# Third and fourth norm of a transformer block by token halves, with the sums of the following modulated norm among the products of a down projection

## What is computed

```
h = layer_norm(ALPHA*h + mix, ln2)
h = layer_norm(ALPHA*h + xa, ln3)                    # xa = cross attention @ wo
h = layer_norm(ALPHA*h + 0.5*swiglu(h, ffn2), ln4)   # 1024 -> 2816 -> 1024
```

```
h2 = rms_norm(h, norm_g) * (1 + scale) + shift       # scale, shift from a condition
z  = h2 @ w_in       # convolutions, neighbourhood attention and gates read it
```

## Time and profile before

| | |
|---|---|
| median of 3 runs | 1752.1 us (1751.47 to 1753.6) |
| profiled execution | 1754.92 us |
| its span | 1753.3 us |
| PE busy | 1719.0 us, 98% |
| DVE busy | 983.3 us, 56% |
| ACT busy | 681.0 us, 39% |
| POOL busy | 149.0 us, 8% |

### The profile page before, as it was taken

One profiled execution on the slowest core, in us unless ns is written; L12 is line 12 of the kernel. 1 busy time (PEld: TensorE's weight loads), 2 busy tenths in 40 slices (PEclk: granted clock), 3 DMA queues, 4 the chain that ended last, 5 costly groups with the idle time before them and its releaser, 6 DMA issues.

```text
span 1753.3 us, 22917 instructions
## 1 busy us (share of the span) xinstructions
PE 1719.0 (98%) x8534; PEld 1409.0 (80%) x8534; DVE 983.3 (56%) x1323; ACT 681.0 (39%) x961; POOL 149.0 (8%) x154
## 2 busy tenths in 40 slices
PE   8999999999999999999999999999999999999999
PEld 7888888788787788886888888876777777788887
DVE  4333339977964674457333333447967769744442
ACT  4222231245445465534222222235444545732221
POOL 0000000012004611012000000003011020000000
PEclk9999999999999999999999999999999999999999
DMA  5332347633221344223333333332332322143331
GB/s 198 96 97 95 99 140 235 221 97 116 73 73 53 128 135 154 61 73 96 101 97 98 98 96 100 96 105 67 92 98 70 96 83 81 61 132 108 108 99 70
DMA packets 50757, 183.87 MB, mean 105 GB/s; under 512 B 5696, under 2 KB 5952, under 8 KB 50304
## 3 DMA queue, kind: packets, MB, share of 16 engines
q1 hardware_dynamic: 44640, 161.50, 29.4%
q10 hardware_dynamic: 5040, 16.00, 2.8%
q0 software_dynamic: 1008, 5.41, 0.9%
HBM read 180.79 MB, written 2.10 MB: 104 GB/s over the span
## 4 chain that ended last, share of the span: by engine, by line
PE 84%; DVE 9%; ACT 2%; DMA 2%; issue 2%; POOL 0%; SPq 0%; ACTq 0%; DVEq 0%
PE proj L372 76%; DVE w_lo L364 2%; DVE ada_prod L1030 1%; DVE y L1851 1%; ACT w_hi L357 1%; PE aux L1696 1%; DMA ctxv<-ada_in 1%; DVE h L645 1%; PE aux L1683 1%; PE aux L1488 1%; PE proj L1509 1%; DMA ctxk<-ada_in 1%; PE aux L1673 1%; DMA h<-x_in 0%; DVE score L1123 0%
## 5 line engine op out<-in xcount | busy, mean ns | idle before, releaser
L364 DVE TENSOR_TENSOR w_lo<-raw,w_hi 128x1024 fp32r<-128x1024 f32 x303 | 383.0, 1265 | 418.4 <-ACT w_hi L357 411.5
L372 PE MATMUL proj<-a_hi,w_hi 128*128 128x512 f32 (+1 forms) x1536 | 603.0, 393 | 9.7 <-DVE a_lo L651 4.4
L372 PE MATMUL proj<-a_hi,w_lo 128*128 128x512 f32 (+1 forms) x1536 | 592.9, 386 | 0.0
L372 PE MATMUL proj<-a_lo,w_hi 128*128 128x512 f32 (+1 forms) x1536 | 592.6, 386 | 0.0
L357 ACT ACTIVATE w_hi<-raw 128x1024 fp32r<-128x1024 f32 x303 | 318.6, 1053 | 233.8 <-PE proj L372 170.8
L372 PEld LDWEIGHTS proj<-a_hi,w_hi 128*128 128x128 f32 x1536 | 289.6, 189 | 76.3 <-DVE a_lo L651 6.6
L372 PEld LDWEIGHTS proj<-a_lo,w_hi 128*128 128x128 f32 x1536 | 290.0, 189 | 58.9 <-issue 2.9
L372 PEld LDWEIGHTS proj<-a_hi,w_lo 128*128 128x128 f32 x1536 | 289.5, 189 | 58.6
L372 PE MATMUL proj<-hid_hi,w_hi 128*128 128x512 f32 (+1 forms) x374 | 142.2, 380 | 0.0
L372 PE MATMUL proj<-hid_hi,w_lo 128*128 128x512 f32 (+1 forms) x374 | 140.8, 377 | 0.0
L372 PE MATMUL proj<-hid_lo,w_hi 128*128 128x512 f32 (+1 forms) x374 | 140.8, 377 | 0.0
(11 more groups left out here) (342 smaller groups left out, 1999.5 us busy)
## 6 DMA issues: line engine op xcount, KB each, us to landing
raw<-stream SPq DMA_DIRECT2D x303, 512.0 KB, 3.5
ctxk<-ada_in ACTq DMA_DIRECT2D x12, 512.0 KB, 3.9
ctxv<-ada_in ACTq DMA_DIRECT2D x12, 512.0 KB, 4.2
out<-h ACTq DMA_DIRECT2D x8, 256.0 KB, 2.0
h<-x_in SPq DMA_DIRECT2D x3, 512.0 KB, 7.6
btab<-rpb_in POOLq DMA_DIRECT2D x4, 384.0 KB, 3.5
cond_row<-cond_in ACTq DMA_DIRECT2D x1, 1024.0 KB, 6.1
side<-mem_in POOLq DMA_DIRECT2D x1, 1024.0 KB, 5.2
```

The source lines that it names most:

```text
L364: nc.vector.tensor_tensor(w_lo[:, st.slot], raw[:, st.slot], w_hi[:, st.slot].bitcast(F32), ALU.subtract).then_inc(lo_ready, 1)
L372: mm = nc.tensor.matmul(dst, a, b, start=start and n == 0, stop=stop and n == 2)
```

## The change

`HALVED` becomes `[0, 4, 5, 6]`: LN3, LN4 and MODN by halves.

- LN3: the last strip of the output projection runs for half 0 and then half 1, with the opening of the sums and the moments of half 0 among the products of half 1; the moments of half 1 stand between the context value strips. The splits of six weight strips are spread anew over the steps of the norm on ACT and VectorE.
- The first four strips of the second feed-forward layer run staggered, half 0 with lags (0, 0, 1, 3), then half 1 with (0, 1, 3, 5).
- LN4: the last chunk of the down projection runs first whole for half 0 (three strips), then whole for half 1, and TensorE takes the first five sums of MODN's half 0 among the products of half 1. The splits of strips 1 and 2 of the next projection move behind that, `ahead=1`.
- MODN by halves: half 0 is normalised while LN4 of half 1 goes on; TensorE takes six of the eight sums of half 1 among the products of half 0 of the next four strips, and two behind them. These run staggered, lags (0, 0, 1, 5) and (0, 1, 3, 5). Their clock-keeping products go.
- `act_na` and `dve_na` split four strips ahead instead of three for j = 0 to 3, and none at j = 4.
- GpSimd adds LN4's shift in sixteen half instructions, each behind the square of its chunk.

The core of the diff:

```diff
-        HALVED = [0]
+        HALVED = [0, 4, 5, 6]
...
+        def act_mod_squares(act, b, lo, hi):
+            for c in range(lo, hi):
+                act.wait_ge(n_xn, LN4.c0 + KD * b + c + 1)
+                if c >= 2:
+                    act.wait_ge(n_stat, MODN.t0 + KD * b + c - 1)
+                nc.scalar.activation(sq[:, c % 2, tokens(b)], h[:, c, tokens(b)], ACT.Square,
+                                     bias=LN4.shift(c)).then_inc(n_sq, 1)
+
+        def pe_mod_stats(pe, b, lo, hi):
+            for c in range(lo, hi):
+                pe.wait_ge(n_sq, MODN.q0 + KD * b + c + 1)
+                nc.tensor.matmul(aux[:, 2 * b + 1, :HT], mean_d[:], sq[:, c % 2, tokens(b)], start=(c == 0),
+                                 stop=(c == KD - 1)).then_inc(n_stat, 1)
...
+        def dve_ln4(dve, b, lo, hi):
+
+            if lo == 0:
+                dve.wait_ge(n_std, LN4.s0 + 2 * b + 1)
+            for c in range(lo, hi):
+                dve.wait_ge(r_cent, 8 * LN4.u + KD * b + c + 1)
+                nc.vector.scalar_tensor_tensor(h[:, c, tokens(b)], h[:, c, tokens(b)], LN4.gain(c), rstd[:, tokens(b)],
+                                               ALU.mult, ALU.mult).then_inc(n_xn, 1)
+                if c + 2 < KD:
+                    dve_half_recentre(dve, LN4, b, c + 2)
+
+        def dve_mod(dve, b, lo, hi):
+
+            if lo == 0:
+                dve.wait_ge(n_std, LN4.s0 + 2 * b + 2)
+            for c in range(lo, hi):
+                if c < KD:
+                    dve.wait_ge(n_raw, LN4.r0 + KD * b + c + 1)
+                    nc.vector.scalar_tensor_tensor(hm[:, c, tokens(b)], h[:, c, tokens(b)], MODN.gain(c),
+                                                   rstd[:, tokens(b)], ALU.mult, ALU.mult).then_inc(mod_xn, 1)
+                if c >= 1:
+                    dve.wait_ge(n_hi, MODN.h0 + KD * b + c)
+                    nc.vector.scalar_tensor_tensor(a_lo[:, c - 1, tokens(b)], hm[:, c - 1, tokens(b)],
+                                                   MODN.shift(c - 1), a_hi[:, c - 1, tokens(b)].bitcast(F32), ALU.add,
+                                                   ALU.subtract).then_inc(n_lo, 1)
...
                 if first and quad:
-                    strip_two_pairs(pe, Nth(s0), Nth(g0), ready)
+                    strips_staggered(pe, Nth(s0), Nth(g0), 0, (0, 0, 1, 3), half_ready_of(pe, ready, 0))
+                    strips_staggered(pe, Nth(s0), Nth(g0), 1, (0, 1, 3, 5), half_ready_of(pe, ready, 1))
...
+            if sums:
+                half(0, 0)
+                half(0, 1)
+                pe_half_open(pe, m)
+                half(0, 2)
+                half(1, 0, {2: lambda: pe_half_mean(pe, m, 0), 4: lambda: pe_half_square(pe, m, 0)})
+                half(1, 1, {5: lambda: sums(0), 7: lambda: sums(1)})
+                half(1, 2, {1: lambda: sums(2), 3: lambda: sums(3), 5: lambda: sums(4)})
+                return
...
                 elif first and j == 0:
-                    strip_two_pairs(pe, st, g, lo_ready_of(pe, MODN))
+                    beside = {n: lambda c=n - 2: pe_mod_stats(pe, 1, c, c + 1) for n in range(2, KD)}
+                    strips_staggered(pe, st, g, 0, (0, 0, 1, 5), half_ready_of(pe, MODN, 0), beside)
+                    pe_mod_stats(pe, 1, KD - 2, KD)
+                    strips_staggered(pe, st, g, 1, (0, 1, 3, 5), half_ready_of(pe, MODN, 1))
...
-                if not first or j:
-                    split_hi(act, st.plus(3))
+                if not first or j != RING:
+                    split_hi(act, st.plus(RING if first and j < RING else 3))
...
+            split_hi(act, Nth(S_CTXV + 2))
+            act_half_square(act, LN3, 0)
+            act_half_mean_square(act, LN3, 0)
+            act_half_std(act, LN3, 0, chain)
+            act_half_hi(act, LN3, 0, 0, 1)
+            split_hi(act, Nth(S_CTXV + 3))
+            act_half_hi(act, LN3, 0, 1, 2)
+            act_half_square(act, LN3, 1)
+            act_half_hi(act, LN3, 0, 2, 3)
+            split_hi(act, Nth(S_FFN2))
+            act_half_mean_square(act, LN3, 1)
+            act_half_hi(act, LN3, 0, 3, 5)
+            split_hi(act, Nth(S_FFN2 + 1))
+            act_half_hi(act, LN3, 0, 5, 6)
+            act_half_std(act, LN3, 1, chain)
+            act_half_hi(act, LN3, 0, 6, 7)
+            split_hi(act, Nth(S_FFN2 + 2))
+            act_half_hi(act, LN3, 0, 7, KD)
             act_ctxv_take(act)
             split_hi(act, Nth(S_FFN2 + 3))
+            act_half_hi(act, LN3, 1, 0, KD)
...
+            for c in range(KD):
+                if c == 2:
+                    split_lo(dve, Nth(S_NA + 3))
+                dve_mod(dve, 0, c + 2, c + 3) if c + 2 <= KD else None
+                dve_ln4(dve, 1, c, c + 1)
+            dve_mod(dve, 1, 0, KD + 1)
...
+            pe_half_strip(pe, last, LN3.groups[KD - 1], 0, a_hi, a_lo, 0, KD, KD)
+            pe_half_strip(pe, last, LN3.groups[KD], 1, a_hi, a_lo, 0, KD, KD,
+                          {0: lambda: pe_half_open(pe, LN3), 3: lambda: pe_half_mean(pe, LN3, 0),
+                           5: lambda: pe_half_square(pe, LN3, 0)})
...
+            pe_down_halves(pe, S_DOWN2, G_DOWN2, KF, LN4, sums=lambda c: pe_mod_stats(pe, 0, c, c + 1))
+            pe_mod_stats(pe, 0, 5, KD)
+            pe_half_mean(pe, LN4, 1)
+            pe_half_square(pe, LN4, 1)
```

More of the change, by code:

```diff
@@ L446, in __init__ @@
                 self.s0 = sum(2 if n in HALVED else 1 for n in range(k))
-                self.c0 = 8 * self.s0
+                self.c0 = 8 * sum(2 if n in HALVED else 1 for n in range(k) if n != 6)
                 self.r = r
@@ L658, in act_hi, with pool_half_shift @@
                 nc.scalar.activation(m.hi[:, c], m.dst[:, c], ACT.Identity, bias=m.shift(c)).then_inc(n_hi, 1)
+        def pool_half_shift(pool, m, after):
+            for b in range(2):
+                for c in range(KD):
+                    pool.wait_ge(n_sq, after.q0 + KD * b + c + 1)
+                    nc.gpsimd.tensor_scalar(h[:, c, tokens(b)], h[:, c, tokens(b)], 1.0, m.shift(c), ALU.mult,
+                                            ALU.add).then_inc(n_raw, 1)
         def pool_shift(pool, m):
@@ L713, in half_ready_of, with pe_half_strip @@
             return lambda k: pe.wait_ge(n_lo, m.h0 + KD * b + k + 1)
-        def pe_half_strip(pe, st, g, b, xh, xl, first, blocks, beside=None):
+        def pe_half_strip(pe, st, g, b, xh, xl, first, blocks, total, beside=None):
             pe.wait_ge(lo_ready, st.n + 1)
@@ L833, in lo_ready_of, with act_mod_hi @@
+        def act_mod_hi(act, b, lo, hi):
+            for c in range(lo, hi):
+                act.wait_ge(mod_xn, KD * b + c + 1)
+                nc.scalar.activation(a_hi[:, c, tokens(b)], hm[:, c, tokens(b)], ACT.Identity,
+                                     bias=MODN.shift(c)).then_inc(n_hi, 1)
         def lo_ready_of(pe, m):
@@ L884, in two @@
                     st, g = Nth(s0 + j, 4, i), Nth(g0 + j, 4, i)
-                    if not (quad and first and j == 0):
+                    if not (quad and first):
                         split_hi(act, st.plus(3))
+                    elif j < 3:
+                        split_hi(act, st.plus(4))
                     if j % 2 == 0:
@@ L904, in two @@
                     st, g = Nth(s0 + j, 4, i), Nth(g0 + j, 4, i)
-                    if not (quad and first and j == 0):
+                    if not (quad and first):
                         split_lo(dve, st.plus(3))
+                    elif j < 3:
+                        split_lo(dve, st.plus(4))
                     if j % 2:
@@ L951, in hybrid_blocks, with act_down_seven @@
         LAST = DOWN_STRIPS * (KD - 1)
-        def act_down_halves(act, s0, m, chain, beside=None):
+        def act_down_seven(act, s0, m, beside=None, ahead=2):
             for a in range(LAST):
@@ L961, in act_down_halves @@
             act_square(act, m, KD - 2)
-            split_hi(act, Nth(s0 + LAST + 4))
+            if ahead == 2:
+                split_hi(act, Nth(s0 + LAST + 4))
+        def act_down_halves(act, s0, m, chain, beside=None):
+            act_down_seven(act, s0, m, beside)
             act_half_square(act, m, 0)
@@ L1878, in dve_na @@
                     norm(2 * (j - 7) + 1)
-                if not first or j:
-                    split_lo(dve, st.plus(3))
+                if not first or j != RING:
+                    split_lo(dve, st.plus(RING if first and j < RING else 3))
                 if j == 2:
@@ L2143, in _ @@
             act_ctxk_norm(act, chain)
-            for n in range(KD):
+            for n in range(KD - 1):
                 split_hi(act, Nth(S_XO + n + 3))
@@ L2163, in _ @@
[L2163 to L2169 removed]
+            act_down_seven(act, S_DOWN2, LN4, ahead=1)
+            act_half_square(act, LN4, 0)
+            act_half_mean_square(act, LN4, 0)
+            act_half_std(act, LN4, 0, chain)
@@ new lines, in _ @@
+            act_mod_squares(act, 0, 0, 2)
```

(18 more changed lines are left out.)

120 lines of the change are left out of this document (62 added, 58 removed).

## The result

The changed kernel takes 1767.55 us (median of 4 runs, 1763.66 to 1769.83), the kernel before beside it 1752.8: a ratio of 1.0083, 95% interval 1.0063 to 1.0102. It is slower by 14.75 us. Its profiled run took 1763.66 us (span 1761.9), the fastest of the four.

The account below looks back on a forecast made before the run. TensorE carries 84% of the chain, but VectorE's slackless chain from the end of strips 0 and 1 sets the kernel's end. Third norm +4.3 and fourth with modulated norm +9.5 sum to +13.8 us: median 1765.9, range 1753 to 1773.

Parts of the forecast that it names:

- both new waits: TensorE waits about 2 us on an add of squares in the output projection, over 3 us at feed-forward strip 2.
- Part one, +2.8 and the clock +1.5: Third norm by halves: late splits and buffer cost 2.8 us, low clock 1.5 (0 to 4.8), together +4.3.
- Part two, the gain: After the modulated norm, the first strip product comes at 1186.3 instead of 1196.89, ten microseconds earlier.
- Part two, half 1: Modulated norm's strips: TensorE idles 2.8 us, starts half 1 at 1207.8, then low clock adds 1.5 us.
- Up to `glu`: VectorE's chain behind the strips: `glu` stands at 1223.6 instead of 1214.44, +9.2 us.
- From `glu` to the scores: VectorE has one split less, -1.1 us, so the wait at 1241.1 moves to 1249.1, +8.0.
- Where TensorE would wait: At the turn behind the first score row, TensorE waits 4 us or more where it waited 0.95.
- (1): Both norm stages: same delays, but the clock stays up; +10.8 us, 1763; chance 0.17.
- (2): Fourth norm: VectorE loses 0.4 us at each of GpSimd's eight half 1 shifts; +3.2 us, 1769; chance 0.08.
- (3): Strips 2 and 3 of both quads: splits and squares reach TensorE in time; -4.5 us, 1747.6; chance 0.08.
- (4): VectorE's chain behind `glu` is absorbed, only the strips' end counts; +4.3 + 1.2 us, 1757.6; chance 0.12.
- (5): Whole kernel: gains and losses cancel within 3.5 us; chance 0.05.

Follow-up runs that it names:

- e1: Only the third norm by halves, the fourth and modulated norms as in the kernel before; 1755.32 us beside 1751.91, ratio 1.0021.
- e4: Changed kernel with the convolution's taps spread over later steps in the first pass; 1762.75 us, ratio 1.0063 to the kernel before.
- e6: Changed kernel with the last two sums of the modulated norm's half 1 among half 0's strip products; 1764.4 us, ratio 1.0064 to before.
- e7: Changed kernel with half 1 of the wide projection's first four strips as two pairs, not staggered; 1767.65 us, ratio 1.0085 to before.
- e9: Changed kernel with small clock-keeping products in TensorE's waits around the modulated norm, strips and first scores; 1764.34 us, ratio 1.0069 to before.
- e2: Only the fourth and modulated norms by halves, the third as in the kernel before; 1761.15 us, ratio 1.0056 to before.
- e12: Changed kernel with paired strips, later splits, earlier last sums, later taps and small clock-keeping products; 1749.27 us beside 1752.55 before, ratio 0.9981.
- e8: Kernel before with six extra VectorE products of nat and nsg ahead of `glu`, first pass only; 1758.06 us beside 1752.34, ratio 1.0030.
- e5: Third norm alone by halves, with half 0 of its four strips as two pairs; 1754.92 us beside 1752.34 before, ratio 1.0013.

## Why the prediction was right, point by point

**The time.** 1766 was predicted, 13.8 us more; measured were 1767.55 and 14.75. The mechanism was right: both new waits, the clock behind most of them, and VectorE's chain as what sets the end of part two. That the sum is so near is in part luck, since in both parts two terms are off in opposite ways, as follows.

**Part one, +2.8 and the clock +1.5.** In the change's own trace A is 3.06 longer, with no drop at the opening. Six profiles have the third norm as the change makes it (change, e1, e4, e6, e7, e9): A is 51.84 to 54.77, mean 53.13, so +4.35, where the prediction had +4.3. The wait at the opening was to be 2.1 and is 1.94; the first strip product was to come 22.65 us behind the chunk's start and comes at 22.68; the wait at strip 2 was to be 4.7 and is 4.52. Only the short wait at strip 3 isn't there. But the split of the sum was off. An estimate from the windows (the missing share of the clock times 4 us each) puts the low clock at 1.7 us in the change and e9, 3.4 in e1, e6 and e7 and 5.1 in e4, a mean of 3.1; without it A would be 49.7 to 50.2, 1.2 above the kernel before. So the walk's +2.8 was 1.6 too much and the clock's +1.5 was 1.6 too little. The run of this part alone, e1, measured +3.4.

**Part two, the gain.** First strip product at 1186.3 by the prediction, 25.15 us behind the chunk's start; measured 25.20. The waits ahead of the strips and at their second step, 1.3 and 0.7 us, are 0.67 and 0.75; the one for the fourth `a_lo`, 2.2, is 2.17.

**Part two, half 1.** The start of half 1 was predicted 46.65 us behind the chunk's start and is 47.93, the wait there 2.59 for 2.8. The step that was too small: I let the clock fall behind the wait at half 1 only, and it also fell behind the one at the fourth `a_lo`, 0.57 in the window from 1192.

**Up to `glu`.** Predicted +9.2, with the clock's 1.5 it is 10.7; measured +12.6. Half 1 slowed down as foreseen (0.67 in the window from 1208). What the sum lacked, beside the 1.3 us at the start of half 1, is GpSimd: its sums for the bias stretch the last split from 1.23 to 1.73 us.

**From `glu` to the scores.** Predicted 1.1 less, measured 2.8 less (86.91 - 65.89 = 21.02 against 23.78), since those same sums were over before most of the taps. The two misses, 1.9 too little and 1.7 too much, nearly cancel. GpSimd's sums are in both, but the 1.3 us of clock has nothing to do with the gain behind `glu`: that these two cancel is luck. The first turn was predicted +8.0 and 1.5 for the clock, and came +10.35 later; at the end of the stage it is +9.86, in e2 +8.64. Predicted: +9.5.

**Where TensorE would wait.** I had it wait some 4 us at the turn. It waits 3.43 at the first scores, half a strip earlier, because `nq` stands behind 14 taps on the same engine. The cause is the chain that I named (e4 takes 8 taps from ahead of `nq`, and the wait goes), the place was wrong. I also had not seen the 3.10 us for `nsq`, behind ScalarE's late `nat`; it is hidden like the rest of TensorE's delay, as e7 shows.

**The rivals.** (1), clock stays up: out, it fell behind the waits of 4.52, 2.59 and 3.43 us, and behind that of 2.17 where I had not put it; in this profile it stayed up behind the opening (1.94 us). e9 shows the price ahead of `glu`. (2), VectorE loses at GpSimd's half shifts: out. GpSimd's shift took 1.14 us beside VectorE and 0.48 alone, while VectorE kept its pace of 0.40 an operation. So the rule that the prediction set beside this rival, by which the one that starts second blocks fully, is not what these rows show:

```profile
1194.79 1.14 POOL L665 TENSOR_SCALAR h<-h,cols 128x256 f32<-128x256 f32 x1 [0.37 <-ACT sq L846]
...
1199.68 0.48 POOL L665 TENSOR_SCALAR h<-h,cols 128x256 f32<-128x256 f32 x1 [0.70 <-ACT sq L846]
```

```profile
1194.80 0.48 DVE L881 SCALAR_TENSOR_TENSOR a_lo<-hm,modv,a_hi 128x256 fp32r<-128x256 f32 x1
1195.20 0.48 DVE L865 SCALAR_TENSOR_TENSOR h<-h,cols,work 128x256 f32<-128x256 f32 x1
```

(3), all splits in time, -4.5: out for this order of work, but e12 shows that the idea could be had, at -3.3, with another order. (4), the chain is absorbed: out by e4 and e8. (5), the parts cancel: out by e1 and e2, both lose.

## What to carry to other kernels

Halving a norm brings the first product forward by as much as one expects, and the end of the strips that somebody is waiting for by nothing. Ask which product the next engine needs, and when the second half of that is done. A wait's releaser in a profile is the last to come; walk the order of the engine behind it before you move anything, or the next wait stands where the old one was (e5). And when a chain of one engine sets the time, look for work in it that can wait, here the taps of a convolution: moving them alone won 1.8 us by the medians in the kernel before (interval -0.2 to 2.8), over half of what the mended version with both norms halved wins.

## What I had not expected of the hardware

**The clock behind the same wait.** The wait of 1.93 to 1.95 us at the opening of the sums is in all nine kernels with the third norm halved. In three of the profiles (change, e9, e12) the granted clock stayed at 1.00 behind it, in the other six the window from 792 shows 0.57 to 0.80, the level of 1.2 GHz for a part of it. With the change's order A is 51.84 and 51.88 in the first kind, 53.35 to 54.77 in the second: 1.5 us or more for nothing that differs in the code there. The wait of 3.10 us for `nsq` is such a case too: a low clock lies around it in e2 (0.73 and 0.84) and follows it in e6 (0.58), and neither in the change nor in e4. The Trainium skill, TensorE: Matmul & The Clock Gate, Part 1, says that the unit that watches TensorE's activity does so in windows that run free of the kernel, so that the same kernel can run more or fewer of its first products at the low clock. These profiles fit that, in mid-kernel; they don't show its cause.

**GpSimd and VectorE beside each other.** With GpSimd's `TENSOR_SCALAR` the loss was all GpSimd's (0.48 to 1.14 us). With its `TENSOR_TENSOR` for the bias both lost: `glu` takes 1.22 us beside them in the change, and 0.69 in the kernel before, where it starts ahead of them; one of GpSimd's takes 0.72 us beside an idle VectorE in the change and 1.19 beside VectorE's products in e8. The Trainium skill, SBUF — State Buffer, section Who interferes with whom, says that a VectorE instruction with two inputs in SBUF contends with a GpSimd instruction that reads SBUF; both cases here are of that kind, and only one of them slowed VectorE.

**The start.** The last chunk of the output projection begins between 784.6 and 789.2 us in these profiles, in code that none of the kernels changed. One profile's end can't be compared with another's; the lengths of its stages can.
